# A two-block transformer kernel on one core: the new residual's square sum from three sums, normalisation by quarters between stages, and heads one piece later

## The reference, cut to what matters

```
h = rmsnorm(x, pre_mix_gain);   proj = h @ w_in                 # 16 heads: 8 stick-breaking, 8 dilated with rope
mix = concat(head_rmsnorm(attention(...)));  x = x + rmsnorm(mix @ w_out, post_mix_gain)
h = rmsnorm(x, pre_ffn_gain);   f = conv_geglu(h @ w_up) @ w_down   # width 5504
x = x + rmsnorm(f, post_ffn_gain)
n = rms_norm(x, mix_norm_g);    z = n @ w_in_2                  # recurrent group and spatial gating group
x = x + concat(a_out, b_out) @ w_out_2
x = x + peer(rms_norm(x, ffn_norm_g), w_q, sub_keys, u, v)      # 8 heads choose 16 of 16384 experts each
out = rms_norm(x, final_norm_g)
rmsnorm(x, g) = x * rsqrt(mean(x * x) + eps) * g
```

## Time and profile before

| | |
|---|---|
| median of 3 runs | 3027.47 us (3021.08 to 3036.96) |
| profiled execution | 3022.35 us, span 3020.7 us |
| TensorE busy | 2894.3 us (96%) |
| VectorE busy | 2152.1 us (71%) |
| ScalarE busy | 1589.9 us (53%) |
| GpSimd busy | 442.2 us (15%) |
| first crossing, TensorE's last matmul to its first next one | 445.17 to 464.96 us |
| second | 1176.85 to 1196.10 us |
| third | 1498.36 to 1509.64 us |

### The profile page before, as it was taken

How to read it: one execution, slowest core, us unless ns; L and a number is a source line. 1 busy time by engine, 2 the same in 40 slices (tenths; PEclk the granted TensorE clock), 3 DMA queues, 4 the chain that set the end, 5 groups by cost and what they waited for, 6 DMA issues and landing times.

```text
span 3020.7 us, 45091 instructions
## 1 busy us (share of the span) xinstructions
PE 2894.3 (96%) x18238; PEld 2611.0 (86%) x18238; DVE 2152.1 (71%) x3244; ACT 1589.9 (53%) x2416; POOL 442.2 (15%) x303
## 2 busy tenths in 40 slices
PE   7999989999999998999898999999999999999998
PEld 6888778888888886998797899998999998999997
DVE  5455557666665445565589899777999777999775
ACT  4477745555554344577443556433556543556533
POOL 0011101222221000133020000133110133110130
PEclk9999999999999999999998999999999999999999
DMA  6534454555556554544564555687666688666784
GB/s 241 181 140 140 141 194 154 185 191 191 187 194 221 191 192 150 200 168 160 196 203 140 188 183 194 241 311 294 241 233 227 230 311 302 237 231 235 272 308 161
DMA packets 99150, 631.43 MB, mean 209 GB/s; under 512 B 11520, under 2 KB 12928, under 8 KB 31360
## 3 DMA queue, kind: packets, MB, share of 16 engines
q1 hardware_dynamic: 80512, 561.43, 52.9%
q0 software_dynamic: 18432, 67.12, 6.2%
HBM read 623.26 MB, written 4.19 MB: 208 GB/s over the span
## 4 chain that ended last, share of the span: by engine, by line
PE 60%; DVE 10%; DMA 10%; issue 3%; ACT 2%; POOL 1%; ACTq 0%; POOLq 0%; DVEq 0%
PE ps L279 24%; PE ps L280 12%; PE ps L1262 5%; DMA ring<-in_v_rows_dram,idx 5%; DMA ring<-in_u_rows_dram,idx 5%; PE ps L301 4%; PE ps L303 4%; PE ps L302 4%; DVE loR L261 3%; PE ps L1264 3%; PE ps L1173 1%; DVE ring L1323 1%; DVE vsum L1330 1%; PE ps L290 1%; PE ps L292 1%
## 5 line engine op out<-in xcount | busy, mean ns | idle before, releaser
L261 DVE TENSOR_TENSOR loR<-raw,hiR 128x1024 fp32r<-128x1024 f32 x1015 | 1248.1, 1237 | 590.6 <-ACT hiR L253 574.8
L253 ACT CAST hiR<-raw 128x1024 fp32r<-128x1024 f32 x1026 | 1073.6, 1050 | 707.1 <-PE ps L1264 317.5
L279 PE MATMUL ps<-XA,hiR 128*128 128x448 f32 (+1 forms) x3936 | 1346.6, 391 | 22.1 <-DVE S__142 L1205 21.6
L280 PE MATMUL ps<-XA,loR 128*128 128x224 f32 (+1 forms) x3936 | 1072.1, 272 | 0.0
L279 PEld LDWEIGHTS ps<-XA,hiR 128*128 128x128 f32 x3936 | 742.6, 189 | 132.0 <-DVE S__142 L1205 23.8
L280 PEld LDWEIGHTS ps<-XA,loR 128*128 128x128 f32 x3936 | 752.2, 191 | 2.5 <-issue 1.9
L1262 PE MATMUL ps<-hl,hiR 128*128 128x448 f32 x2048 | 650.1, 377 | 11.5 <-DVE loR L261 11.3
L1264 PE MATMUL ps<-hl,loR 128*128 128x224 f32 x2048 | 542.8, 265 | 0.0
L1262 PEld LDWEIGHTS ps<-hl,hiR 128*128 128x128 f32 x2048 | 384.4, 188 | 49.0 <-DVE loR L261 15.6
L1264 PEld LDWEIGHTS ps<-hl,loR 128*128 128x128 f32 x2048 | 391.3, 191 | 0.2 <-issue 0.2
L1301 POOL DMA_INDIRECT ring<-in_u_rows_dram,idx x64 | 102.6, 1604 | 733.3 <-DVE ring L1323 672.0
(11 more groups left out here) (284 smaller groups left out, 3506.2 us busy)
## 6 DMA issues: line engine op xcount, KB each, us to landing
raw<-in_u_dram SPq DMA_DIRECT2D x128, 1024.0 KB, 4.9
raw<-in_v_dram SPq DMA_DIRECT2D x128, 1024.0 KB, 5.5
raw<-in_w_up_dram SPq DMA_DIRECT2D x86, 1024.0 KB, 4.9
raw<-in_w_down_dram SPq DMA_DIRECT2D x43, 1024.0 KB, 4.9
raw<-in_w_in_qk_dram SPq DMA_DIRECT2D x32, 1024.0 KB, 4.9
raw<-in_w_out_dram SPq DMA_DIRECT2D x32, 1024.0 KB, 4.9
raw<-in_w_in_dram SPq DMA_DIRECT2D x24, 1024.0 KB, 4.9
raw<-in_w_in_v_dram SPq DMA_DIRECT2D x16, 1024.0 KB, 4.9
```

The source lines that it names most:

```text
L253: e.copy(hiR[:, r:r + 2, :], raw[n % NR][:, q:q + 2, :]).then_inc(S("hi"), 1)
L261: e.tensor_tensor(loR[:, r:r + 2, :], raw[n % NR][:, q:q + 2, :], hiR[:, r:r + 2, :].bitcast(F32), ALU.subtract).then_inc(S("lo_pool" if p ...
L279: e.matmul(both, wh, X.hl[:, :, k, 0:nt], start=(k == 0), stop=False, skip_group_check=True)
L280: m = e.matmul(dst[:, 0:nt], wl, X.h[:, k, 0:nt], start=False, stop=(k == KC - 1), skip_group_check=True)
```

## The change

- The square sum of the new x is no longer taken from the new x. With x' = x + r f, the sum is S(x x) + r S(2 x f) + r r S(f f). `dve_cross` and `act_cross` make the last two sums per quarter; three of four quarters in the stage before the crossing (steps 36, 42, 54 of the w_out stage), the last behind the evacuation. S(x x) is the sum that the normalisation before has left. Five tiny operations on VectorE put them together.
- `act_out_square` begins with token half 0, which need not wait for VectorE; the evacuation waits for one square instead of two.
- x is updated a quarter at a time, mixed with the scaling. TensorE turns one quarter (two at the start and in the third crossing) and begins with its pieces; the later turns stand between pieces (`TURN_AT`). For that the first 4 column blocks of w_up and the first 2 of w_q are laid out and used quarter by quarter (`UPQ`, `QQ`).
- The splits of pieces 4 to 11 stand between the steps of the normalisation; the FFN's own work starts 12 steps later (`FFN0`).
- While TensorE waits it makes products of the identity (at the start of zeros), `pe_keep`: 36 + 10, 30 + 6, 30 + 6 and 16 + 6, into a bank that is free.
- The table of the square root is loaded ahead of time by a dummy activation, `act_sqrt_table`.
- Every head step but the turn by `perm` and the rotary sum moves one piece later; the last key sum moves ahead of a split.
- The first two of GpSimd's splits of the query stage go to VectorE. A few semaphores are merged.

```
     g = 2 * u
-    if P_Q <= g < P_U[0]:
+    if P_Q + 12 <= g < P_U[0]:
         return u % 3 == 0
...
+    TURN_FIRST = [2, 1, 1, 2]
+    TURN_AT = [{4: 2, 8: 3}, {2: 1, 6: 2, 10: 3}, {2: 1, 6: 2, 10: 3}, {2: 2, 4: 3}]
+    KEEP = [(36, 10), (30, 6), (30, 6), (16, 6)]
+    def pe_keep(e, i, n, b):
+        for _ in range(KEEP[i][n]):
+            a = warm if (i, n) == (0, 0) else ident
+            e.matmul(bank[b][:, 0:128], a[:, :], a[:, :], start=True, stop=True)
+    def pe_norm_first(e, i, b):
+        pe_keep(e, i, 0, b)
+        if i == 0:
+            e.wait_ge(S("ident"), 16)
+        for q in range(TURN_FIRST[i]):
+            pe_norm_turn(e, i, q)
+        pe_keep(e, i, 1, b)
...
-        e.wait_ge(S("fsq"), 8 * i + 2 * fb + 2)
+        e.wait_ge(S("fsq"), 8 * i + 2 * fb + 1)
         e.tensor_tensor(out_fo[i][:, 0, cs], bank[out_banks[i][fb][0]][:, :], out_gain[i][:, cs],
...
+    def dve_cross(e, i, fb):
...
+            e.scalar_tensor_tensor(junkx[i][:, tb, :], x[:, tb, cs], 2.0, out_fo[i][:, tb, cs], ALU.mult, ALU.mult,
+                                   accum_out=st[:, c:c + 1]).then_inc(S("sxf"), 1)
+    def act_cross(e, i, fb):
...
+            e.activation(junkf[i][:, :], out_fo[i][:, tb, quarter(fb)], ACT.Square,
+                         accum_out=st[:, c:c + 1]).then_inc(S("sff"), 1)
...
+    def act_branch(e, i, end):
         col = out_col[i]
+        e.wait_ge(S("piece"), end)
+        act_out_square(e, i, 3)
+        e.wait_ge(S("part"), 1 + i)
         act_root(e, 1 + 2 * i, st[:, col + 8:col + 14])
+        act_cross(e, i, 3)
+        e.wait_ge(S("quad"), 5 * i + 5)
         act_root(e, 2 + 2 * i, st[:, col + 24:col + 30])
+        split_hi(e, end + 6)
+        act_norm_hi(e, 1 + i, 0)
+        act_norm_hi(e, 1 + i, 1)
+        split_hi(e, end + 8)
+        act_norm_hi(e, 1 + i, 2)
+        split_hi(e, end + 10)
+        act_norm_hi(e, 1 + i, 3)
...
-            elif d == 4:
+            elif d == 5:
                 e.wait_ge(S("dl_add"), h + 1)
...
-        for q in range(4):
-            pe_norm_turn(e, 1, q)
-        for j in range(2 * NF):
+        e.wait_ge(S("fo"), 6)
+        e.wait_ge(S("fsq"), 6)
+        pe_norm_first(e, 1, 0)
+        for n in range(4 * UPQ):
+            q, j = divmod(n, UPQ)
+            pe_norm_next(e, 1, n)
...
+            wide(e, P_UP + n, q, XA, bank[j], T)
+        for j in range(UPQ, 2 * NF):
...
         e.activation(tmp0[:, 0, :], x[:, 0, :], ACT.Square, accum_out=ss[:, 0:1]).then_inc(S("x0sq"), 1)
-        split_hi(e, 0)
         e.wait_ge(S("x0sq"), 1)
         e.wait_ge(S("x1sq"), 1)
-        e.wait_ge(S("cst"), 2)
         act_root(e, 0, ss)
+        act_norm_hi(e, 0, 0)
+        split_hi(e, 0)
         split_hi(e, 2)
-        for q in range(4):
-            act_norm_hi(e, 0, q)
+        act_norm_hi(e, 0, 1)
+        split_hi(e, 4)
+        split_hi(e, 6)
+        act_norm_hi(e, 0, 2)
+        split_hi(e, 8)
+        act_norm_hi(e, 0, 3)
         e.wait_ge(S("start_const"), 48)
         e.activation(lz[:, 16:32], lv[:, 72:88], ACT.Abs).then_inc(S("lam_a"), 1)
```

More of the change, by code:

```diff
@@ L400, in dve_branch @@
+    def dve_branch(e, i, end):
+        col, c = out_col[i], sum_col[i]
+        dve_out_evac(e, i, 3, end)
         e.wait_ge(S("fsq"), 8 * i + 8)
         dve_sum_parts(e, 1 + 2 * i, col)
+        dve_cross(e, i, 3)
         dve_root(e, 1 + 2 * i, st[:, col + 8:col + 14])
-        e.wait_ge(S("fo"), 8 * i + 8)
-        for tb in range(2):
-            for fb in range(4):
-                cs = quarter(fb)
-                e.scalar_tensor_tensor(x[:, tb, cs], out_fo[i][:, tb, cs], st[:, col + 12 + tb:col + 13 + tb],
-                                       x[:, tb, cs], ALU.mult, ALU.add).then_inc(S("xb"), 1)
@@ new lines, in dve_branch @@
+        for tb in range(2):
+            r = st[:, col + 12 + tb:col + 13 + tb]
+            e.wait_ge(S("quad"), 5 * i + tb + 2)
+            e.scalar_tensor_tensor(st[:, col + 24 + tb:col + 25 + tb], st[:, c + 20 + tb:c + 21 + tb], r,
+                                   sum_x[i][:, tb:tb + 1], ALU.mult, ALU.add).then_inc(S("quad"), 1)
+        dve_x_new(e, i, 0, 1)
+        dve_root(e, 2 + 2 * i, st[:, col + 24:col + 30])
+        dve_norm_scale(e, 1 + i, 0)
+        dve_x_new(e, i, 1, 0)
+        dve_norm_lo(e, 1 + i, 0)
@@ L415, in act_branch @@
+        dve_x_new(e, i, 1, 1)
+        dve_norm_scale(e, 1 + i, 1)
+        for tb in range(2):
+            dve_x_new(e, i, 2, tb)
+        dve_norm_lo(e, 1 + i, 1)
+        split_lo(e, end + 6)
+        dve_norm_scale(e, 1 + i, 2)
+        split_lo(e, end + 8)
+        dve_x_new(e, i, 3, 0)
+        dve_norm_lo(e, 1 + i, 2)
+        dve_x_new(e, i, 3, 1)
+        split_lo(e, end + 10)
+        dve_norm_scale(e, 1 + i, 3)
+        dve_norm_lo(e, 1 + i, 3)
+    def act_branch(e, i, end):
         col = out_col[i]
-        e.wait_ge(S("part"), 1 + 2 * i)
+        e.wait_ge(S("piece"), end)
+        act_out_square(e, i, 3)
+        e.wait_ge(S("part"), 1 + i)
@@ L1573, in act_program @@
                 e.wait_ge(S("piece"), P_DN + n)
-                act_out_square(e, 1, n // NF - 1, P_DN + n)
-        e.wait_ge(S("piece"), P_GV)
-        act_out_square(e, 1, 3, P_GV)
-        act_branch(e, 1)
-        for q in range(4):
-            act_norm_hi(e, 2, q)
+                act_out_square(e, 1, n // NF - 1)
+            if n % NF == 8 and n > 8:
+                act_cross(e, 1, n // NF - 1)
+            if n == 60:
+                act_sqrt_table(e, 2)
+        split_hi(e, P_GV + LA)
+        act_branch(e, 1, P_GV)
         for n in range(32):
-            split_hi(e, P_GV + n + LA)
+            if n + LA >= 12:
+                split_hi(e, P_GV + n + LA)
             if n == 16:
@@ L1594, in act_program @@
                 act_x2_square(e, WO2_END.index(n - 1))
+        split_hi(e, P_Q + LA)
         act_x2_square(e, 3)
-        e.wait_ge(S("part"), 5)
+        e.wait_ge(S("part"), 3)
         act_root(e, 5, st[:, 96:102])
-        for q in range(4):
+        for q in range(3):
             act_norm_hi(e, 3, q)
+        split_hi(e, P_Q + 6)
+        act_norm_hi(e, 3, 3)
         for s in range(64):
-            split_hi(e, P_Q + s + LA)
+            if s + LA >= 8:
+                split_hi(e, P_Q + s + LA)
             act_choice(e, s)
@@ L1624, in act_program @@
         act_x_square(e, 3)
-        e.wait_ge(S("part"), 6)
+        e.wait_ge(S("part"), 4)
         act_root(e, 6, st[:, 128:134])
```

308 lines of the change are left out of this document (187 added, 121 removed).

## The result

| | before | after |
|---|---|---|
| median, us (lowest to highest) | 3029.48 (3021.08 to 3036.96) | 2991.76 (2987.50 to 3002.21) |
| executions | 4 | 4 |
| profiled execution: time / span | 3022.35 / 3020.70 | 2987.50 / 2986.21 |

The ratio after to before is 0.9893, with a 95% interval of 0.9858 to 0.9928: the changed kernel is faster by 1.1%. A second set of executions gave 0.9906 (0.9882 to 0.9931), with medians of 2995.27 and 3022.05. The forecast was 2990, from 2976 to 3009.

What follows compares the result with a forecast made beforehand. TensorE, busy 2894.3 of 3020.7 us, was taken as the bound, with waits at start, crossings and heads to remove. Terms summed to 37.0 us (bounds 20 and 43), giving 2990 us, range 2976 to 3009.

Steps and rivals of the forecast that it cites:

- start: Beginning of the kernel: first matmul at 16.4 instead of 25.96 us, two turns and one stall after; gain 7.2 us, bounds 4 to 9.5.
- heads and last key sum: Key/query stage: later head steps cover TensorE's wait for GpSimd's rotary sum, 9.9 us; key sum ahead of a split, 2.7.
- output stage (evacuation): Shorter evacuation before the third output quarter: 1.63 us of wait less 1.26, gain 1.3 us, bounds 0.5 to 1.6.
- first crossing: Output stage to up projection: first up matmul at 9.4 instead of 19.79 us, gain 7.8 us at piece 16, bounds 5 to 9.
- second crossing, to piece 16, and behind it: Same chain at the second stage boundary, gain 6.0 us, bounds 3.5 to 7.5; late weights behind mixer constants costed at nothing.
- third crossing: Boundary before the queries: TensorE starts after quarter 0 instead of quarter 3; gain 2.1 us, bounds 0 to 3.
- the stall behind the Abs and the table load: Early pieces: split of pieces 10 and 11 waits on ScalarE behind casts, Abs and Exp; TensorE loses 2.2 us.
- Rival 4: VectorE's queue decides at the crossings: piece 12 waits 3 us at both; gain 30 us, 2997; chance 0.12.
- Rival 1: Identity products don't hold the clock, which falls to 0.50 at crossings; gain only 10 us, 3017; chance 0.12.
- signs of being wrong: Clock at 0.50 in a crossing, a new TensorE wait for a split in the heads, or products ending after the scaled half.
- rival 2: Heads keep their wait because ScalarE's queue is late, not GpSimd's sum; gain 24 us, 3003; chance 0.10.
- rival 3: Heads' sixteen ln/exp blocks, 3.5 us each, delay the splits: 56 us against 37, slower at 3047; chance 0.04.

## Why the prediction was right, and where not

The forecast of 2990 against 2991.76 is closer than its terms were. In the first profiled pair, 37.0 us were forecast and 34.5 measured:

| term | forecast | measured |
|---|---|---|
| start | 7.2 | 7.3 |
| heads and last key sum | 9.9 + 2.7 | 6.2 |
| output stage (evacuation) | 1.3 | 1.6 |
| first crossing | 7.8 | 7.8 |
| second crossing, to piece 16, and behind it | 6.0 | 6.7 - 1.7 |
| third crossing | 2.1 | 2.1 |
| expert phase | 0 | 4.5 |

- **Start, first and third crossing: right, step by step.** First matmul forecast 16.4, came at 16.39; the stall behind the Abs and the table load forecast 2.2 us, came at 1.83; first up matmul 9.4 and 9.33. Piece 12 was forecast at 29.4 behind the last output matmul, held 0.5 by its split, and came at 29.31, held by it as forecast:

```profile
PE ps L286 <- DVE loR L268: 0.3, 1, 0.3
...
456.57 1.29 DVE L352 TENSOR_TENSOR XA<-ps,XA 128x512 fp32r<-128x512 f32 x2 [2.01 <-ACT XA L346]
```

  But it is not the length of VectorE's queue that decides. VectorE stood idle for 2.01 us ahead of quarter 3's lower part and waited for ScalarE's cast behind the third turn; turn, cast, lower part and split are the chain, and taking six updates out of VectorE's queue (old square sum) left the 16 pieces at 25.61. Rival 4 fell: piece 12 did not wait 3 us. The 7.8 us are made up so: the scaling starts 5.57 us earlier (10.81 to 5.24), from there to the first up matmul it takes 4.09 instead of 8.98, and the 16 pieces take 2.67 more. Of the 5.57, the run with the old sum gives the three sums 3.87; the other 1.70, evacuation order and preloaded table, stand in no run of their own, and neither does the quarter-wise start. In the stall the table load and the exp behind it stand as forecast from the rows, 1.28 us and then 0.02, without the 1.38 of a drain that the Trainium skill (ScalarE: Activation LUTs, What ACT_TABLE_LOAD costs) adds:

```profile
29.89 0.23 ACT L1658 ACTIVATE lz<-lv 128x16 f32<-128x16 f32 x1
30.13 1.28 ACT L1660 ACT_TABLE_LOAD   x1
31.43 0.22 ACT L1660 ACTIVATE lz<-lz 128x16 f32<-128x16 f32 x1
31.55 3.88 ACT L260 CAST hiR<-raw 128x1024 fp32r<-128x1024 f32 x4
```

- **The clock: right.** Without the products 6.8 to 8.4 us are lost. I forecast 0.7 a crossing for it in the pieces; it is 1.5 and 2.8. Rival 1, products too short to hold the clock, did not happen. One of my signs of being wrong did come: the products end after the scaled half, which was there 0.6 us earlier than forecast, and that costs 0.35 us a crossing.
- **Heads: the step that failed.** I wrote that the ln/exp blocks would "stand behind a split instead of ahead of one" and cost nothing, and looked at their length only. For the dilated heads that is so. For the stick-breaking heads it is the other way round: their logarithm stood behind a copy and a split and now stands ahead of them, so it found the ones product missing and waited 2.7 us with a split and a key/query copy behind it. TensorE waited 6.6 us for that, and the whole stage lost 9.6. Without this fault the stage gains 15.8 us (236.62 to 220.84) where I had summed up 12.6, with it 6.2; where the other 3.2 come from was not followed. The wait for GpSimd did vanish, 9.9 us, as forecast, so rival 2 fell; rival 3 had the right place and far too high a price (1.1 to 1.4 us a head instead of 3.5 a block). The last key sum was worth 1.15 of its 2.7: with the step moved, 1.4 of the wait stayed, and 2.3 in the changed kernel.
- **Second crossing: the bound named it, the sum left it out.** The constants for the mixer did come late, "1 to 2 us if they come late": ScalarE's first split behind them waited 8.23 us for its raw tile:

```profile
1192.45 1.05 ACT L260 CAST hiR<-raw 128x1024 fp32r<-128x1024 f32 x1 [8.23 <-DMA raw<-in_w_gv_dram]
```

  The run with the constants behind the fetches gave the 1.73 us back.
- **Expert phase: not the forecast's doing.** The 4.5 us there stand against a spread of 1403.5 to 1411.7 over the changed kernel and its variants, and of 3.7 us between two profiles of the kernel before. Whether a part is the change's stays open.
- **Up stage: not foreseen at all.** In its second profile and in every variant the changed kernel loses 8.7 us there. With it the first pair would have differed by 26 us, which is near what the medians of the second timing show (26.8, where those of the first show 37.7 and I forecast 37). Which pace the executions without a profile had is not known. That the first median lies so near the forecast owes something to luck.

## What to carry to other kernels

Where a stage boundary is one chain, take out of it what can be summed earlier: at two crossings the three sums were worth 8.9 us, the clock's part included. Starting the next stage on the first quarter and interleaving the rest goes with it; the 16 pieces behind hardly waited, but no run shows what that is worth alone. Give TensorE products that nobody reads while it waits: 6.8 to 8.4 us over the start and three pauses, at two of the pauses mostly earned in the pieces behind them, while at the third they cost 0.3 us. When steps of a hand-written order are moved, check on each in-order engine which moved instruction now reaches the head of the queue before its producer, even when both moved by the same number of pieces, and what stands behind it: one product a piece earlier was worth 9.6 us, more than the whole move had brought.

## What the chip showed beyond that

**Two paces of the same stream.** In the up stage TensorE alternates 512- and 256-column products without a wait, at a granted clock of 1.00. In the first profile of the changed kernel, then in the second, records of the same pair of lines over 100 us:

```profile
L286 PE MATMUL ps<-XA,hiR 128*128 128x512 f32 x289 | 100.2, 391 | 0.0
L287 PE MATMUL ps<-XA,loR 128*128 128x256 f32 x289 | 80.9, 280 | 0.0
```

```profile
L286 PE MATMUL ps<-XA,hiR 128*128 128x512 f32 x285 | 100.7, 399 | 0.0
L287 PE MATMUL ps<-XA,loR 128*128 128x256 f32 x284 | 79.8, 281 | 0.0
```

A piece takes 1386.7 ns or 1413.3 ns, 1.9% more, and a pace once begun lasts to the end of the stage: 8.7 us. In all twelve profiles with transposes between the pieces, the pieces behind the second and third turn were at 1386.7. Behind the wait for the weights of pieces 12 and 13, eleven of those twelve were at 1413.3 or so; the kernel before has no wait there and was at 1386.7 twice. It looks as if the restart picks the pace, but four transposes did not bring the quick one back, and behind the first turn either pace came. Nor does it need a wait or the change: all fourteen profiles, the kernel before's too, begin the key/query stage at the slow pace (pieces of 1410, 1410 and 1421 ns) without a wait of TensorE there. The chip alone does not pick it either, since the second profiles of the two kernels were taken on one chip and differ. What picks it is open; the wait at piece 12 was not taken away.
